# Score banks released one at a time, whole-row exponentials, and other queues for the router's stores

## Chip, cores and metric

One core of one Trainium2 chip runs the whole program. The metric is the time of one execution in device microseconds (us). The kernel before took 4668.68 us, the median of 3 runs (4661.94 to 4672.85).

## What is computed

A transformer block with latent attention, dilated attention and a 16-expert feed-forward, followed by two layers that hold three attentions each; width 1024, 1024 tokens, in later layers 256 context tokens more. All in float32. What the change touches is softmax attention and the router:

```python
s = einsum('bqhd,bkhd->bhqk', q, k) * scale        # scores of 128 queries against 1024 or 1280 keys
p = softmax(s, axis=-1)
o = einsum('bhqk,bkhd->bqhd', p, v)
...
h2 = rms_norm(x, g_ffn) * (1.0 + sc_m) + sh_m      # the router's features, gathered later by the experts
aff = softmax(einsum('bsd,de->bse', h2, w_router) + b_router)
gate, idx = top_k(swapaxes(aff, 1, 2), cap)        # each of 16 experts chooses 128 tokens
x = x + gt_m * expert_choice_ffn(h2, ...)
```

## The kernel before

The program is a row of stages; each is a block with its own instruction list per engine, and a barrier stands between two blocks.

**stage_attention** (from L891) is called five ways. Its names in the trace are `am` (latent attention, 1024 keys), `ad` (dilated attention, 1024 keys, with a bias), `aa` (difference maps, 1280 keys), `ab` (grouped queries, 1280 keys) and `ac` (neighbourhood, `apart=True`, up to 384 near keys and 256 context keys, with a bias). `aa`, `ab` and `ac` run once in each of the two layers. A step `h` is one head and one tile of 128 queries. Its scores lie in the PSUM buffer `ps[h % SB]` of `banks` banks of 512 columns. With 1024 keys `banks` is 2, `SB` (buffers) is 3 and `LAG` is 2; with 1280 keys `banks` is 3, `SB` is 2 and `LAG` is 1. Steps with all 1024 or 1280 keys number 64 in `am`, 64 in `ad`, 128 in `aa` and 96 in `ab` (both layers together); in the first of the two layers `aa` and `ab` also have short steps, for the context queries, with 256 keys.

What one step does, engine by engine. PE: `scores(h)` (L1052), then `transposes(h - LAG)` (L1062), which turns the probabilities 128 columns at a time back into the same PSUM buffer, then in every second step `turned` (L1087, one transpose), then half of `values` (L1078). DVE: in every second step the part that ends a pair of heads (L1127 to L1136: add the two partial denominators, reciprocal, two multiplications), then the row maximum of step h (L1146; in `ad` the bias and the maximum in one, L2226), then its share of copying the turned probabilities of step h - LAG from PSUM to `pT` (L1117). ACT: in every second step a copy of `po` to `oT` (L1161), then its share of the copy to `pT` (L1167), then two exponentials of step h, one for each of the two `spans` (L1178), each with a read of the accumulated denominator.

The spans are (0, 512) and (512, width). ACT copies `by_act`: the columns up to `(banks - 1) * 512`, so 512 of 1024 and 1024 of 1280, and in `ad` all 1024. DVE copies the rest, `by_dve`: 512 in `am`, 256 in `aa` and `ab`, none in `ad`. `scores(h)` overwrites the buffer of step h - SB, so it waits ahead of its first matmul for both copies of that step, `eva` (ACT) and `evd` (DVE), at L1047 and L1048. DVE credits `evd` after its copy, and in program order that copy stands behind the maximum of the step after next (`am`, `ad`) or the next (`aa`, `ab`). `transposes` waits for the first exponential (`ex0`, L1058) and ahead of column 512 for the second (`ex`, L1061); `tr0` tells ACT that its columns are turned, `tr` tells DVE.

**stage_router** (from L1339) goes over 8 tiles of 128 tokens. SP loads 8 weight chunks of 2 MB into 3 buffers (L1379) for a product with the conditioning that shares the stage (`mod_product`, L253). DVE makes the features `h2[:, t % 2]` of a tile (L1419, L1422), PE turns them (L1452), ACT copies them (L1397), PE forms the logits (L1462), ACT and DVE the softmax. The features of tile t reuse the buffer of tile t - 2, so DVE first waits for that tile's store (L1418). Both stores go out from POOL's queue, in this order for each tile: the store of `h2` to `h2_d` (L1475; `h_d` in the trace), a wait until it has landed (L1476), the store of the same tile of `x_sb` to `x_d` (L1477). The latter turns tokens into grid order: a tile is 2 grid rows of 64 tokens, and the transfer is [2 rows][64 tokens][1024], with tokens 64 KB apart in `x_d`. Nothing in the stage reads `x_d`; the block ends when all has landed (L1479). The stage after it, `stage_choose`, picks tokens on DVE.

## Time and profile before

| | |
|---|---|
| median of 3 runs | 4668.68 us |
| the profiled execution | 4670.11 us, of which the span is 4668.2 us |
| PE busy | 3658.2 us (78%) |
| DVE busy | 2452.2 us (53%) |
| ACT busy | 2213.7 us (47%) |
| POOL busy | 921.1 us (20%) |
| mean granted TensorE clock | 0.898 of full |
| `am`, `ad` | 492 to 765 us, 785 to 1035 us |
| router stage | 1141 to 1297 us |
| `aa`, `ab`, first of the two layers | 2475 to 2800, 2800 to 3050 us |
| `aa`, `ab`, last layer | 3890 to 4122, 4122 to 4342 us |

The profile shows the chip's own record of one execution. A busy share is an average over stages with different limits, so each stage is read alone: in the timeline of a few steps one looks for the work before which an engine sat idle, and for what released it (in brackets at a row's end). PE is TensorE's matmuls, PEld its weight loads, DVE VectorE, ACT ScalarE, POOL GpSimd; "ACTq L1182" as a releaser means ACT's queue at that line. The clock is 1.00 at TensorE's upper level, 2.4 GHz, and 0.50 at its lower, 1.2 GHz.

### The profile page before, as it was taken

The page shows a single profiled execution, that of the slowest core. Times are in us where ns is not written, and L with a number is a line of the kernel's source. Part 1 is how long each engine was busy: PE and PEld are TensorE (multiplying, and loading weights), DVE is VectorE, ACT ScalarE, POOL GpSimd, SP SyncE. Part 2 cuts the span into 40 slices and gives each one's busy share as a digit, 9 for nine tenths or more (in the row PEclk, how much of TensorE's full clock was granted, in tenths as well). Part 3 has the DMA queues.
Part 4 walks back from the last instruction along what each step waited for, and adds up shares of the span by engine and source line. Part 5 has one row for each costly group of instructions (what it writes and reads, how often), then busy time and mean ns, then how long its engine had stood idle before and what let it go on. Part 6 is the DMA issues. An engine that isn't in the chain of part 4 may idle for free. (4 is left out here: it accounts for less than half of the span.)

```text
span 4668.2 us, 70984 instructions
## 1 busy us (share of the span) xinstructions
PE 3658.2 (78%) x24823; PEld 2986.7 (64%) x24823; DVE 2452.2 (53%) x4546; ACT 2213.7 (47%) x3912; POOL 921.1 (20%) x748
## 2 busy tenths in 40 slices
PE   3987786888339999769996868865979968869558
PEld 3974565667327888558874657643768856658446
DVE  2114454443268878557544545555558745546455
ACT  2216454761017777542225656645442217657452
POOL 0214000000005656315550000000025540000002
PEclk7998898998669999879998989987989989989889
DMA  7237413412469999633323314061233332232433
GB/s 253 78 113 223 111 38 81 109 34 91 154 250 359 398 394 397 233 124 108 104 75 72 104 41 109 20 146 59 72 128 108 108 97 52 82 80 61 97 102 91
DMA packets 332951, 625.03 MB, mean 134 GB/s; under 512 B 122148, under 2 KB 178372, under 8 KB 331556
## 3 DMA queue, kind: packets, MB, share of 16 engines
q1 hardware_dynamic: 291360, 506.26, 34.2%
q0 software_dynamic: 39776, 108.71, 7.6%
q8 instruction: 209, 3.42, 0.3%
q10 hardware_dynamic: 1444, 5.30, 0.3%
q14 instruction: 162, 1.33, 0.1%
HBM read 486.20 MB, written 133.97 MB: 133 GB/s over the span
## 5 line engine op out<-in xcount | busy, mean ns | idle before, releaser
L1941 PE MATMUL pr_ps<-pr_wH,hT_part 128*128 128x512 f32 (+1 forms) x1120 | 428.6, 383 | 0.0
L1693 ACT ACTIVATE ex_high<-ex_ring 128x2048 fp32r<-128x2048 f32 x192 | 368.7, 1920 | 96.7 <-PE ex_pg L1669 41.2
L1739 DVE TENSOR_TENSOR ex_ring_part<-ex_ring,ex_high 128x2048 fp32r<-128x2048 f32 x144 | 372.9, 2589 | 51.4 <-ACTq L1694 39.6
L1941 PE MATMUL pr_ps<-pr_wH,x_sb_part 128*128 128x512 f32 x896 | 359.2, 401 | 20.9 <-DVEq L2017 20.9
L1941 PE MATMUL pr_ps<-pr_ws_part,x_sb_part 128*128 128x512 f32 x896 | 352.9, 394 | 0.0
L1146 DVE TENSOR_REDUCE aa_nm<-aa_ps 128x1 f32<-128x1280 f32 (+1 forms) x144 | 197.7, 1373 | 228.3 <-PE aa_ps L1052 227.6
L1634 POOL TENSOR_TENSOR ex_ring_part<-ex_ring,ex_high 128x2048 fp32r<-128x2048 f32 x48 | 239.5, 4989 | 217.2 <-ACTq L1694 217.2
L1062 PE MATMUL aa_ps<-ident,aa_prob 128*128 128x128 f32 x1312 | 208.6, 293 | 60.3 <-ACTq L1182 59.1
L1178 ACT ACTIVATE aa_prob<-aa_ps,aa_nm 128x512 f32<-128x512 f32 (+2 forms) x272 | 210.9, 775 | 87.6 <-DVEq L1147 45.4
L1146 DVE TENSOR_REDUCE ab_nm<-ab_ps 128x1 f32<-128x1280 f32 (+1 forms) x108 | 148.3, 1373 | 194.4 <-PE ab_ps L1052 193.9
L1941 PEld LDWEIGHTS pr_ps<-pr_wH,hT_part 128*128 128x128 f32 x1120 | 211.3, 189 | 44.6
L1262 PE MATMUL o_ps<-o_wH,o_yT 128*128 128x512 f32 x832 | 230.7, 395 | 0.0
L1062 PEld LDWEIGHTS aa_ps<-ident,aa_prob 128*128 128x128 f32 x1312 | 148.9, 147 | 112.7 <-ACTq L1182 106.1
L1941 PEld LDWEIGHTS pr_ps<-pr_wH,x_sb_part 128*128 128x128 f32 x896 | 169.4, 189 | 57.1 <-DVEq L2012 21.8
L1178 ACT ACTIVATE ab_prob<-ab_ps,ab_nm 128x512 f32<-128x512 f32 (+1 forms) x204 | 158.4, 776 | 95.7 <-DVEq L1147 69.9
L1941 PEld LDWEIGHTS pr_ps<-pr_ws_part,x_sb_part 128*128 128x128 f32 x896 | 169.5, 189 | 34.1
L1052 PE MATMUL ac_ps<-ac_kT,ac_qT 128*128 128x384 f32 (+1 forms) x204 | 75.0, 372 | 146.6 <-DVEq L1118 84.2
L1052 PE MATMUL aa_ps<-aa_kT,aa_qT 128*128 128x512 f32 (+1 forms) x400 | 121.8, 413 | 82.7 <-DMA aa_v<-proj 64.3
L1167 ACT ACTIVATE aa_pT<-aa_ps 128x1024 f32<-128x1024 f32 (+1 forms) x144 | 137.1, 952 | 83.0 <-PE aa_ps L1062 82.4
L1078 PE MATMUL aa_po<-aa_pT,aa_v 128*64 128x128 f32 x2624 | 176.4, 280 | 0.0
L1262 PEld LDWEIGHTS o_ps<-o_wH,o_yT 128*128 128x128 f32 x832 | 156.0, 190 | 31.4
L1178 ACT ACTIVATE ac_prob<-ac_ps,ac_nm 128x384 f32<-128x384 f32 (+1 forms) x204 | 104.3, 511 | 145.7 <-DVEq L1147 135.3
(358 smaller groups left out, 9001.6 us busy)
## 6 DMA issues: line engine op xcount, KB each, us to landing
ex_ring<-in_w_gate SPq DMA_DIRECT2D x64, 1024.0 KB, 10.2
ex_ring<-in_w_up SPq DMA_DIRECT2D x64, 1024.0 KB, 8.7
ex_ring<-in_w_down SPq DMA_DIRECT2D x64, 1024.0 KB, 8.4
z_d<-pr_zT POOLq DMA_DIRECT2D x120, 256.0 KB, 3.1
pr_ws<-in_w_in SPq DMA_DIRECT2D x14, 2048.0 KB, 9.1
mod_w<-in_w_ada SPq DMA_DIRECT2D x10, 2048.0 KB, 13.2
rt_mw<-in_w_ada SPq DMA_DIRECT2D x8, 2048.0 KB, 13.4
proj<-pr_raw POOLq DMA_DIRECT2D x54, 256.0 KB, 2.3
```

The costliest lines, as they stand in the source:

```text
L1052: mm = tensor.matmul(ps[h % SB][:, at:at + m], q.bitcast(F32R), kk.bitcast(F32R), start=i == 0, stop=i == len(ab) - 1)
L1062: mm = tensor.transpose(ps[h % SB][:, c:c + P], prob[:, h % SB, c:c + P], ident[:, :])
L1078: mm = tensor.matmul(po[j * dv:(j + 1) * dv, 0:P], v[:, p % 2, key, j * dv:(j + 1) * dv], pT[:, m % 2, j, at:at + P], start=c == 0, stop=c ...
L1146: vector.tensor_reduce(most, ps[h % SB][:, 0:count[t]], AX.X, ALU.max, negate=True)
L1167: scalar.activation(pT[:, g // 2 % 2, j, cols], ps[g % SB][:, cols], ACT.Copy)
L1178: scalar.activation(prob[:, h % SB, c0:c1], ps[h % SB][:, c0:c1], ACT.Exp, bias=nm[:, h % SB:h % SB + 1], scale=-1.0 if add_bias is not No ...
L1262: mm = tensor.matmul(ps[:, t % 2, cols], yT[:, t % 2, part, c, :].bitcast(F32R), w[:, c, cols].bitcast(F32R), start=c == 0 and i == 0, sto ...
L1634: pool.tensor_tensor(w_part[:, c % SL].bitcast(F32R), w_sb[:, c % SL], wH[:, c % HL], ALU.subtract)\
L1693: scalar.activation(wH[:, c % HL].bitcast(F32R), w_sb[:, c % SL], ACT.Copy)
L1739: vector.tensor_tensor(w_part[:, c % SL].bitcast(F32R), w_sb[:, c % SL], wH[:, c % HL], ALU.subtract)
L1941: mm = tensor.matmul(ps[:, g % 4, c0:c1], x.bitcast(F32R), w[:, i % WS, kk, c0:c1].bitcast(F32R), start=kk == 0 and m == 0, stop=kk == KC ...
```

## The change

Five edits to attention and two to the router.

1. The wait for `evd` moves from ahead of all of `scores(h)` to ahead of its columns from 512 on, where ACT's share is exactly columns 0 to 512 (`am`, `aa`, `ab`). Elsewhere (`ad`, `ac`, short steps) it stays ahead of the first matmul and is repeated ahead of each piece.
2. `by_act` with 1280 keys shrinks from 1024 columns to 512; DVE's share grows from 256 to 768.
3. New spans for the exponentials, `rises`: with 3 buffers (`am`, `ad`) one exponential of 1024; with 1280 keys one of 1024 and one of 256, in place of 512 and 768. `ac` keeps its two.
4. `transposes` waits for `ex` where the second rise starts: at column 1024 with 1280 keys, and not at all in `am` and `ad`.
5. The addition of two denominators (L1127) is dropped where there is one rise.
6. The router's `h2` stores go out from ACT's queue, after the copy of the turned features, with a semaphore for each of the two buffers.
7. The stores to `x_d` stay on POOL's queue, but are issued at once after `gd` (L1413), without a wait between them, 16 of one grid row each: [64 tokens][1024], 256 KB.

```diff
--- before.py
+++ after.py
@@ -931,10 +931,14 @@
         SB = 6 // banks
         LAG = SB - 1
 
+
+        rises = [s if apart or len(s) == 1 else [(0, s[-1][1])] if SB == 3 else
+                 [(0, (banks - 1) * 512), ((banks - 1) * 512, s[-1][1])] for s in spans]
+
         def by_act(t):
             if len(spans[t]) == 1 or (add_bias is not None and not apart):
                 return (0, spans[t][-1][1])
-            return spans[t][0] if apart else (0, (banks - 1) * 512)
+            return spans[t][0] if apart else (0, 512)
 
         def by_dve(t):
             c0, c1 = by_act(t)[1], spans[t][-1][1]
@@ -1043,10 +1047,12 @@
                         p, t, j = steps[h]
                         if t == 0 and j == 0:
                             pe.wait_ge(ld[p % 2], turn(it, p) * 16 * (n_loads + 2))
+
                         if h >= SB:
                             pe.wait_ge(eva, it * n + (h - LAG))
-                            pe.wait_ge(evd, it * n + (h - LAG))
                         for at, key, m in pieces(t):
+                            if h >= SB and (at == 512 or by_act(t) != (0, 512)):
+                                pe.wait_ge(evd, it * n + (h - LAG))
                             ab = passes(p % 2, j, t * P, key, m)
                             for i, (q, kk) in enumerate(ab):
                                 mm = tensor.matmul(ps[h % SB][:, at:at + m], q.bitcast(F32R), kk.bitcast(F32R),
@@ -1057,7 +1063,7 @@
                         t = steps[h][1]
                         pe.wait_ge(ex0, it * n + (h + 1))
                         for c, _ in chunks(t):
-                            if len(spans[t]) == 2 and c == spans[t][1][0]:
+                            if len(rises[t]) == 2 and c == rises[t][1][0]:
                                 pe.wait_ge(ex, it * n + (h + 1))
                             mm = tensor.transpose(ps[h % SB][:, c:c + P], prob[:, h % SB, c:c + P], ident[:, :])
                             if c + P == by_act(t)[1]:
@@ -1123,7 +1129,7 @@
                         if g % 2 and g >= 5:
                             m = (g - 5) // 2
                             p, t, _ = steps[2 * m]
-                            if len(spans[t]) == 2:
+                            if len(rises[t]) == 2:
                                 vector.tensor_tensor(den[:, m % RING, 0, :], den[:, m % RING, 0, :], den[:, m % RING, 1, :], ALU.add)
                                 dve.drain()
                             vector.reciprocal(rd[:, :], den[:, m % RING, 0, :])
@@ -1173,8 +1179,8 @@
                             if m >= RING:
                                 act.wait_ge(od, it * M + (m - RING + 1))
                             for x in range(2):
-                                if x < len(spans[t]):
-                                    c0, c1 = spans[t][x]
+                                if x < len(rises[t]):
+                                    c0, c1 = rises[t][x]
                                     scalar.activation(prob[:, h % SB, c0:c1], ps[h % SB][:, c0:c1], ACT.Exp,
                                                       bias=nm[:, h % SB:h % SB + 1],
                                                       scale=-1.0 if add_bias is not None else 1.0,
@@ -1341,8 +1347,9 @@
 
         n = "rt"
         ld, var, root, gd, kept = (sem(f"{n}_{s}") for s in ("ld", "var", "root", "gd", "kept"))
-        h_full, t_full, hT_full, lg, soft, ex, at_full, at_out, st, soft_out = (
-            sem(f"{n}_{s}") for s in ("h", "t", "hT", "lg", "max", "ex", "aT", "aTo", "st", "so"))
+        h_full, t_full, hT_full, lg, soft, ex, at_full, at_out, soft_out = (
+            sem(f"{n}_{s}") for s in ("h", "t", "hT", "lg", "max", "ex", "aT", "aTo", "so"))
+        st = [sem(f"{n}_st{j}") for j in range(2)]
 
         chunks = MOD_ROUTER
         NM = len(chunks)
@@ -1396,11 +1403,14 @@
                         act.wait_ge(lg, t)
                     scalar.activation(hT[:, :, :], tp[:, :, :], ACT.Copy)
                     act.drain().then_inc(hT_full, 1)
+                    act.dma_start(h2_d[t * P:(t + 1) * P, :], h2[:, t % 2, :]).then_inc(st[t % 2], 16)
                     act.wait_ge(soft, t + 1)
                     if t:
                         act.wait_ge(at_full, t)
                     scalar.activation(aff[:, :], lgt[:, :], ACT.Exp, bias=nm[:, 0:1], accum_out=den[:, 0:1])
                     act.drain().then_inc(ex, 1)
+                for j in range(2):
+                    act.wait_ge(st[j], 16 * (ST // 2))
 
             @block.vector
             def _(dve):
@@ -1415,7 +1425,7 @@
                 def features(t):
                     b = t % 2
                     if t >= 2:
-                        dve.wait_ge(st, 16 * (t - 1))
+                        dve.wait_ge(st[t % 2], 16 * (t // 2))
                     vector.scalar_tensor_tensor(h2[:, b, :], x_sb[:, t * D:(t + 1) * D], r[:, t:t + 1], gb[:, :],
                                                 ALU.mult, ALU.mult)
                     dve.drain()
@@ -1470,13 +1480,11 @@
             @block.gpsimd
             def _(pool):
                 pool.wait_ge(gd, 1)
-                for t in range(ST):
-                    pool.wait_ge(h_full, t + 1)
-                    pool.dma_start(h2_d[t * P:(t + 1) * P, :], h2[:, t % 2, :]).then_inc(st, 16)
-                    pool.wait_ge(st, 16 * (t + 1))
-                    pool.dma_start(x_d.rearrange("(c r) d -> r c d", r=ROWS)[t * P // GRID:(t + 1) * P // GRID],
-                                   x_sb[:, t * D:(t + 1) * D]).then_inc(kept, 16)
-                pool.wait_ge(kept, 16 * ST)
+                for r in range(ROWS):
+                    t, half = r // (P // GRID), r % (P // GRID)
+                    pool.dma_start(x_d.rearrange("(c r) d -> r c d", r=ROWS)[r],
+                                   x_sb[half * GRID:(half + 1) * GRID, t * D:(t + 1) * D]).then_inc(kept, 16)
+                pool.wait_ge(kept, 16 * ROWS)
 
     EX_RING = 11
```

## Rows read from the trace of the kernel before

**Rows 1.** Stretches: us, busy time by engine, granted clock, DMA share, GB/s

```profile
1141.00:1297.00 156.00, 56.11 (x712) 49.43 (x712) 33.69 (x72) 14.49 (x29) 11.02 (x16) 0.62 0.51 173
1271.00:1290.00 19.00, 0.00 (x0) 0.00 (x0) 0.00 (x0) 0.00 (x0) 0.82 (x1) 0.50 0.13 40
2500.00:2625.00 125.00, 107.09 (x1032) 80.93 (x1030) 69.99 (x136) 89.91 (x181) 0.97 (x1) 1.00 0.15 33
```

**Rows 2.** Router timeline: start us, us, engine, line, operation, [idle before <-releaser]

```profile
1163.37 3.09 PE L253 MATMUL rt_mp<-rt_mw,mod_c 128*32 128x128 f32 x64
...
1171.71 3.64 PE L253 MATMUL rt_mp<-rt_mw,mod_c 128*32 128x128 f32 x64
...
1184.67 0.56 POOL L1475 DMA_DIRECT2D h_d<-rt_h  x1
...
1201.10 1.28 DVE L1419 SCALAR_TENSOR_TENSOR rt_h<-x_sb,rt_r,rt_g 128x1024 f32<-128x1024 f32 x1 [9.52 <-DMA h_d<-rt_h]
```

**Rows 3.** Router timeline, its end

```profile
1260.71 1.95 PE L253 MATMUL rt_mp<-rt_mw,mod_c 128*32 128x128 f32 x64
...
1282.27 0.82 POOL L1477 DMA_DIRECT2D x_d<-x_sb  x1 [13.76 <-DMA h_d<-rt_h]
...
1297.77 0.39 SPq L1524 DMA_DIRECT2D ch_mw<-in_w_ada  x1
```

**Rows 4.** DMA issues of the page, POOL's queue: count, KB each, us to landing

```profile
proj<-pr_raw POOLq DMA_DIRECT2D x54, 256.0 KB, 2.3
```

**Rows 5.** Waits in am: for whom, us in total, times, longest

```profile
PE am_ps L1052 <- DVEq L1118: 18.6, 56, 1.4
```

**Rows 6.** Timeline of am, one round of the loop that sets its pace

```profile
605.81 1.63 PE L1052 MATMUL am_ps<-am_kT,am_qT 96*128 96x512 f32 x6 [0.34 <-DVEq L1118]
...
607.48 1.23 DVE L1146 TENSOR_REDUCE am_nm<-am_ps 128x1 f32<-128x1024 f32 x1 [1.84 <-PE am_ps L1052]
...
608.82 0.69 DVE L1117 COPY am_pT<-am_ps 128x512 f32<-128x512 f32 x1
...
609.68 1.63 PE L1052 MATMUL am_ps<-am_kT,am_qT 96*128 96x512 f32 x6 [0.24 <-DVEq L1118]
```

**Rows 7.** Instructions by tile: duration ns min/median/max, first and last start, forms

```profile
L1178 ACT ACTIVATION_READ_ACCUMULATOR am_prob<-am_ps,am_nm x128: 190/193/195, 497.6 to 749.8; 128x1 f32 x128
...
L1178 ACT ACTIVATE aa_prob<-aa_ps,aa_nm x272: 473/690/902, 2482.5 to 4111.0; 128x512 f32<-128x512 f32 x128, 128x256 f32<-128x256 f32 x8
```

**Rows 8.** Timeline of ad, two steps

```profile
852.99 0.19 PEld L1052 LDWEIGHTS ad_ps<-ad_kT,ad_qT 128*128 128x128 f32 x1 [0.35 <-ACTq L1168]
...
855.40 1.02 ACT L1167 ACTIVATE ad_pT<-ad_ps 128x1024 f32<-128x1024 f32 x1
...
856.66 0.19 PEld L1052 LDWEIGHTS ad_ps<-ad_kT,ad_qT 128*128 128x128 f32 x1 [0.17 <-ACTq L1168]
...
858.76 1.02 ACT L1167 ACTIVATE ad_pT<-ad_ps 128x1024 f32<-128x1024 f32 x1 [0.46 <-PE ad_ps L1062]
```

**Rows 9.** Timeline of aa, two steps

```profile
2600.93 0.85 PE L1052 MATMUL aa_ps<-aa_kT,aa_qT 128*128 128x512 f32 x3
...
2603.68 0.42 DVE L1117 COPY aa_pT<-aa_ps 128x256 f32<-128x256 f32 x1 [0.37 <-PE aa_ps L1062]
...
2605.82 1.49 DVE L1146 TENSOR_REDUCE aa_nm<-aa_ps 128x1 f32<-128x1280 f32 x1 [0.55 <-PE aa_ps L1052]
...
2606.65 0.87 PE L1062 MATMUL aa_ps<-ident,aa_prob 128*128 128x128 f32 x6 [0.43 <-ACTq L1182]
...
2607.34 1.02 ACT L1167 ACTIVATE aa_pT<-aa_ps 128x1024 f32<-128x1024 f32 x1 [0.77 <-PE aa_ps L1062]
...
2608.70 0.86 PE L1052 MATMUL aa_ps<-aa_kT,aa_qT 128*128 128x512 f32 x3
```

**Rows 10.** Timeline of ab: the first matmul of scores, two steps apart

```profile
2901.30 0.50 PE L1052 MATMUL ab_ps<-ab_kT,ab_qT 128*128 128x512 f32 x1
...
2908.94 0.50 PE L1052 MATMUL ab_ps<-ab_kT,ab_qT 128*128 128x512 f32 x1
```

## Prediction

> **What bounds the kernel now.** I read the stretches first, because the change touches stages with different limits, and then in each stage a timeline of two or three steps, looking for the idle time ahead of an engine's work and its releaser.
>
> The router stage takes 156 us, PE is busy for 56 of them, the DMA engines for half, at a clock of 0.62 [rows 1]. It is a chain of stores. POOL issues the store of one tile's features at 1184.67, and DVE starts the features of the next tile but one at 1201.10, after 9.52 us of idleness that ended when that store landed [rows 2]: one tile in 16 to 18 us. Why is a store of 512 KB so slow? At 1282.27 the last store to `x_d` goes out, into an empty machine, and the next stage starts at 1297.77 [rows 3]; from 1271 to 1290 the DMA share is 0.13 at 40 GB/s [rows 1]. That is 2 engines of 16. So the `x_d` store of a tile, shaped [2][64][1024], is cut in two and takes some 14 us whatever else goes on, and the feature store of the next tile stands behind it in POOL's queue.
>
> In `am` one loop closes: scores 1.63, 0.04 to the maximum, 1.23, 0.11, the copy 0.69, 0.17, scores again, 3.87 us in all [rows 6]. PE idles for the end of that copy 56 times, 18.6 us in total [rows 5]. In `ad` ACT and PE pass the step to each other: ACT's copy takes 1.02 and scores start 0.08 to 0.24 after it, at 856.66; the next copy starts 2.10 later [rows 8]. The other step, from 852.99 to 856.66, is 3.67 long because its copy starts only 2.41 after the scores, ACT being busy with exponentials and `oT`. In `aa` two steps take 7.77 us, 3.885 each [rows 9]. ACT goes round: exponentials of 512 and 768, wait 0.77 for the turned columns, copy 1024. PE waits 0.43 for the second exponential in each step. DVE has room. In `ab` two steps take 7.64 us, 3.82 each, and scores start with no idle time ahead of them [rows 10]: scores have two passes there, and PE is the bound.
>
> **The change, part by part.**
>
> Router, edits 6 and 7. Three chains remain. First the tiles themselves. Where no store held them back, product 0 to product 1 took 8.34 us (1163.37 to 1171.71) [rows 2]: DVE's two feature operations, PE's transposes, the product, and DVE's row sum, all at a low clock. The product took 3.09 and 3.64 there but 1.95 at the end, once PE had been busy for a while [rows 2, 3]. I take 8.0 us. Six such rounds and a shorter one of 5 (it makes no features: 8.0 less two operations like the 1.28 of [rows 2] and their gaps) put product 7 at 1163.4 + 48 + 5 = 1216.4. Before it stood at 1260.7 [rows 3]. From there to the end of the block I allow 6 us for the last row sum, four small stores and the barrier: 1222. Second the `x_d` stores. A 256 KB store on POOL's queue lands in 2.3 us in another stage [rows 4], so 16 of them are tens of microseconds of one sixteenth-spread queue, beside 6 MB of weights; they are over by about 1180. Third the `h2` stores. Each goes out about a copy of 1024 columns after its transposes (1.02 in `ad` [rows 8]), and its buffer is wanted 13 us after them (features t + 2), so it has over 11 us; nothing is ahead of it on ACT's queue, and what is behind it is the softmax's exponential, for which ACT now idles anyway. An issue costs 0.56 on POOL [rows 2]; the trace has none of this size on ACT, so 0 to 0.8 us each, on no path. The one thing that could hurt is the flood at the start: 4 MB of stores on top of 6 MB of weights. I allow 2 us. The block then ends at 1224 in place of 1297.8: **74 us less**, 62 to 84 by tile rounds of 9.0 or 6.5 us and 0 to 4 us for the flood.
>
> The Trainium skill, "DMA: Bandwidth & Descriptors", section on why a DMA increments its semaphore by 16, says that the number of DMA engines is the largest up to 16 that divides the slowest dimension of both sides: 2 before, 16 after. The share of 0.13 [rows 1] agrees for the old shape; no row has the new one. The same page, "Issuing engines are not separate DMA queues", speaks against edit 6: moving a store to another issuer saves issue time only. By that rule alone edit 6 would give nothing; the rows show the time lost in the order within POOL's queue and its narrow neighbour, which edits 6 and 7 both end.
>
> `am`, edits 1, 3, 5. The first half of scores no longer waits for DVE, so PE's 18.6 us go [rows 5]. What is late next is PE. DVE's loop now holds half the scores: 0.82 + 0.04 + 1.23 + 0.11 + 0.69 + 0.17 = 3.06, under PE's own 3.87 less some 0.3, 3.55. One exponential of 1024 delays the first transposes of a step, but they come two steps later. It shortens ACT, which isn't late. **18 us**, 8 to 20.
>
> `ad`, edits 3, 5. The waits stay. Exponentials of 256, 512 and 768 take 473, 690 and 902 ns [rows 7], 0.212 us for each 256 columns, so 1024 take 1.115. Two of 512 and two reads of the accumulator (0.193) become one and one: 1.38 + 0.39 - 1.115 - 0.19 = 0.46 us less on ACT per step. In the long step ACT's copy then starts when the columns are turned, 2.10 after the scores as in the other step, and scores follow at 3.2 to 3.3 in place of 3.67 [rows 8]. In the short step ACT waits 0.46 for PE already, and nothing is won. 0.39 us in each of 32 pairs: **12 us**, 0 to 14.
>
> `aa`, edits 1 to 4. Four durations are new. Copies on DVE: 256 columns take 0.42 [rows 9], 512 take 0.69 [rows 6], so 768 take 0.96. ACT's copy falls from 1.02 to about 0.6. The exponentials keep their sum (512 + 768 = 1024 + 256), and the last one no longer stands between PE and most of its transposes: those of eight chunks need only the first. So PE's 0.43 and ACT's 0.77 [rows 9] both shrink, and ACT leaves the path. DVE comes onto it. Even step: the 768 columns of scores that wait, 0.57 (0.85 for 1280 [rows 9] less 0.28 for the first 512, an estimate by columns), 0.04, maximum 1.49, 0.11, copy 0.96, 0.17, together 3.34. Odd step: DVE does the pair's end between copy and maximum. It takes 1.17 now (from 2604.10, the copy's end, to 2605.27, where the 0.55 of idleness begin [rows 9]); 1.49 + 0.11 + 0.96 + 1.17 + 0.1 = 3.83. The pair is 7.17, 3.585 a step. PE needs 7.77 - 0.86 = 6.91 and stays under that. 0.30 us in 128 steps: **38 us**; the two ends are PE's own bound, 0.43 each and 55 us, and 17 us if the early first bank brought nothing (rivals).
>
> `ab`, the same edits. PE has little idle time to give, a tenth of a microsecond in some steps at the `ex` wait by my estimate. DVE's loop: the waiting part of scores is 768 columns twice, as much as the half of `am`'s, 0.82; with the 2.77 of everything behind it 3.59 in the even step, 3.83 in the odd one, 3.71 together, below 3.82 but by 0.11 only. **3 us**, from a loss of 10 to a gain of 8. `ac` gets one satisfied wait more per step, ahead of a matmul queued behind a running one: 0, up to a loss of 3.
>
> Sum against the profiled execution: 74 + 18 + 12 + 38 + 3 = 145; 4670.1 - 145 = **4525 us**. That execution was 1.4 us above the median shown, so the same number stands for the median.
>
> **Rivals.**
>
> A, DVE takes the bound in `aa` and `ab` entirely. If starting the first bank early brings nothing (the matmuls of a step are held together by something else), the loop has all the scores again: `aa` 0.85 + 2.77 = 3.62 and 3.83, mean 3.73, so 20 us are won instead of 38; `ab`, five sixths of `am`'s scores, 1.36 + 2.77 = 4.13, a loss of 0.31 in 96 steps, 30 us. Time 4525 + 18 + 33 = 4576. For it: DVE's margin in `ab` is 0.11 us. Against it: nothing in the program ties the banks together.
>
> B, the `x_d` stores don't spread. If a store of one grid row uses two engines again, 16 of them in one queue still need 8 times 14 = 112 us from ten microseconds before product 0 on, and the block ends at 1266: 32 us won in place of 74, 4567 us. This is the case in which edit 7 doesn't do what it says. Against it: the store of [rows 4] with many outer rows lands in 2.3 us.
>
> C, more than forecast: PE runs at the upper level in the router (rounds of 6.5 us, 9 us more) and is the bound in `aa` (17 more): 4499.
>
> D, slower than before. The clock: it stands at 1.00 in `aa` with PE busy 107 of 125 us, and at 0.62 in the router with 56 of 156 [rows 1]. If PE, now waiting in the middle of scores on top of ahead of transposes, were granted 0.50 in attention, a step of 3.8 us with some 3.4 of PE work would take about 7, 3.2 more. It decides from 45 such steps of 352 on (145 / 3.2). Against it: PE's waits get shorter in total, not longer.
>
> **How the numbers follow.** Forecast 0.74, A 0.09, B 0.07, C 0.09, D 0.01. Own ranges: the terms' ends added as independent errors give about 25 us to each side of 4525. The range takes in B and A: 4492 to 4582. About 0.2% (9 us) is what a measurement of this kernel can tell from no change. Every case but D is far beyond that: faster 0.98, same 0.01, slower 0.01.
>
> **What would show it.** In the router: eight rounds of 7 to 9 us, no DVE wait for `h_d`, a block of some 83 us, and `x_d` stores landing within 30 us of the first issue. In `am`: no wait for L1118 left, steps of 3.55 to 3.6. In `ad`: both steps 3.2 to 3.3. In `aa`: steps of 3.34 and 3.83, DVE's copy 0.96, and a PE wait for DVE's copy in the middle of scores. In `ab`: 3.8 as before. The prediction is wrong if the router's gain is under 60 us, or if `ab` becomes slower than 3.9 a step.

## The result, and the profile after

The changed kernel takes 4503.37 us, the median of 4 runs (4501.89 to 4505.05), beside 4666.97 us for the kernel before on the same chip; the ratio is 0.9649, with a 95% interval of 0.9632 to 0.9666. The forecast was 4525 us, its range 4492 to 4582. The profiled execution took 4502.05 us, 168.1 less than the one shown of before, where the sum of the prediction said 145. Of all executions below one ran in a slower state of the chip (`split_same_reg`, 4923.15 us at a granted clock of 0.749); no figure includes it.

Busy times on the page of the changed kernel (engine, us, share of the span, instructions):

```profile
span 4499.9 us, 70349 instructions
PE 3621.7 (80%) x24823; PEld 2979.1 (66%) x24823; DVE 2568.7 (57%) x4482; ACT 2074.7 (46%) x3656; POOL 922.5 (20%) x748
```

ACT gives 139 us of work away, DVE takes 117 more. PE's share hardly moves; what goes is idle time. Where it goes is read stage by stage. For an attention stage the figure is the time from the start of its first row maximum to that of its last (in `ac` of the first layer, to the last with near keys). For the router it is the time from the issue of the block's first load to the issue of the next block's first load of large weights. Digits 0 and 1 are the first and the last layer. The figures are taken from the profiled executions, one of each kernel; a gain is worked out before rounding.

| stage | before | after | gain | forecast |
|---|---|---|---|---|
| `am` | 251.3 | 231.9 | 19.4 | 18 |
| `ad` | 227.3 | 212.0 | 15.3 | 12 |
| router | 156.2 | 81.9 | 74.2 | 74 |
| `aa` 0 + 1 | 548.0 | 509.9 | 38.2 | 38 |
| `ab` 0 + 1 | 386.9 | 376.4 | 10.5 | 3 |
| `ac` 0 + 1 | 303.5 | 299.6 | 3.9 | 0 |
| all the rest | 2795.0 | 2788.2 | 6.8 | 0 |

**Router.** Stretches of the block in the changed kernel; the columns are those of [rows 1], the last two the DMA share and GB/s:

```profile
1115.00:1125.00 10.00, 6.07 (x28) 5.70 (x29) 5.36 (x6) 2.32 (x3) 8.48 (x16) 0.50 1.05 390
1125.00:1135.00 10.00, 8.55 (x160) 7.48 (x159) 4.13 (x10) 2.84 (x6) 0.00 (x0) 0.88 1.03 413
...
1155.00:1165.00 10.00, 8.49 (x122) 7.50 (x114) 5.49 (x11) 1.43 (x3) 0.00 (x0) 0.83 1.05 395
1165.00:1183.00 18.00, 14.62 (x243) 12.75 (x243) 7.59 (x21) 3.25 (x8) 0.00 (x0) 0.81 0.59 228
```

Against 0.51 of [rows 1] the DMA share is 1.03 to 1.05 for fifty microseconds. The tail at a share of 0.13 is gone. The products of its timeline on PE:

```profile
1126.18 2.54 PE L253 MATMUL rt_mp<-rt_mw,mod_c 128*32 128x128 f32 x64
...
1133.09 1.96 PE L253 MATMUL rt_mp<-rt_mw,mod_c 128*32 128x128 f32 x64
...
1143.86 3.64 PE L253 MATMUL rt_mp<-rt_mw,mod_c 128*32 128x128 f32 x64 [3.51 <-DMA rt_mw<-in_w_ada]
...
1180.27 1.96 PE L253 MATMUL rt_mp<-rt_mw,mod_c 128*32 128x128 f32 x64
```

Eight products, 54.1 us from the first to the last start. DVE waits for no `h_d` any more; PE waits once, for weights. The `x_d` stores, from the view of the DMA issues in that stretch:

```profile
L1485 POOL DMA_DIRECT2D x_d<-x_sb x16: 532/539/578, 1115.2 to 1123.2; - x16
...
DMA to landing us min/median/max: 6.6/11.4/18.5
```

**`am`.** Two steps of the timeline (start, duration, engine, line, what waited for what); compare [rows 6]:

```profile
640.68 1.23 DVE L1152 TENSOR_REDUCE am_nm<-am_ps 128x1 f32<-128x1024 f32 x1 [0.55 <-PE am_ps L1058]
...
642.02 0.69 DVE L1123 COPY am_pT<-am_ps 128x512 f32<-128x512 f32 x1
...
642.47 1.66 PE L1058 MATMUL am_ps<-am_kT,am_qT 96*128 96x512 f32 x6
...
644.16 1.23 DVE L1152 TENSOR_REDUCE am_nm<-am_ps 128x1 f32<-128x1024 f32 x1 [1.45 <-PE am_ps L1058]
...
647.76 1.23 DVE L1152 TENSOR_REDUCE am_nm<-am_ps 128x1 f32<-128x1024 f32 x1 [0.52 <-PE am_ps L1058]
```

Scores at 642.47 start while DVE's copy, 642.02 to 642.71, still runs. The maxima are 3.48 and 3.60 apart, in place of 3.87. The wait for DVE's copy (L1118 in [rows 5], L1124 now) has no row left among PE's waits in the stage.

**`ad`.** Maxima at 860.67 and 863.92, 3.25 apart. Over the stage they are 3.20 and 3.29 apart in turn, in place of 3.67 and 3.21 around [rows 8]:

```profile
860.67 1.23 DVE L2234 CUSTOM_DVE_ANT_0 ad_ps<-ad_ps,logc 128x1024 f32<-128x1024 f32 x1 [1.93 <-PE ad_ps L1058]
...
861.39 1.02 ACT L1173 ACTIVATE ad_pT<-ad_ps 128x1024 f32<-128x1024 f32 x1 [0.20 <-PE ad_ps L1068]
...
862.54 0.50 PE L1058 MATMUL ad_ps<-ad_kT,ad_qT 128*128 128x512 f32 x1
...
863.92 1.23 DVE L2234 CUSTOM_DVE_ANT_0 ad_ps<-ad_ps,logc 128x1024 f32<-128x1024 f32 x1 [0.95 <-PE ad_ps L1058]
```

ACT's copy now waits 0.20 for the turned columns: here ACT has stopped being late.

**`aa`, last layer.** DVE's timeline over a pair, and PE's row of the second part of scores:

```profile
3811.86 0.61 PE L1058 MATMUL aa_ps<-aa_kT,aa_qT 128*128 128x512 f32 x2 [0.54 <-DVEq L1124]
...
3812.51 1.49 DVE L1152 TENSOR_REDUCE aa_nm<-aa_ps 128x1 f32<-128x1280 f32 x1 [0.73 <-PE aa_ps L1058]
...
3814.12 0.96 DVE L1123 COPY aa_pT<-aa_ps 128x768 f32<-128x768 f32 x1
...
3815.20 0.16 DVE L1133 TENSOR_TENSOR aa_den<-aa_den 128x2 f32<-128x2 f32 x1
...
3815.76 0.48 DVE L1142 TENSOR_SCALAR aa_o<-aa_pf,aa_rd 128x64 f32<-128x64 f32 x2 [0.16 <-issue]
...
3816.43 1.49 DVE L1152 TENSOR_REDUCE aa_nm<-aa_ps 128x1 f32<-128x1280 f32 x1 [0.19 <-issue]
...
3819.74 1.49 DVE L1152 TENSOR_REDUCE aa_nm<-aa_ps 128x1 f32<-128x1280 f32 x1 [0.74 <-PE aa_ps L1058]
```

The two steps are 3.92 and 3.31. The maximum at 3816.43 waits for nothing but DVE itself, because the end of the pair stands ahead of it: DVE has come onto the path, as forecast. PE now waits 0.54 in the middle of scores, for DVE's copy (L1124).

**`ab`.** DVE's maxima (2759.89, 2763.55, 2767.39) are 3.66 and 3.84 apart, over the whole stage 3.70 and 3.80; before 3.70 and 3.93.

### The profile page after: what moved, and what is told of

Its sections match the earlier page's. It is cut to its first block and busy times, and to the rows that moved or that the text cites. A ratio compares the mean times of both kernels' runs of the same rounds, so it can differ in the third digit from the quotient of the medians.

```text
span 4499.9 us, 70349 instructions
## 1 busy us (share of the span) xinstructions
PE 3621.7 (80%) x24823; PEld 2979.1 (66%) x24823; DVE 2568.7 (57%) x4482; ACT 2074.7 (46%) x3656; POOL 922.5 (20%) x748
## 5 line engine op out<-in xcount | busy, mean ns | idle before, releaser
L1184 ACT ACTIVATE aa_prob<-aa_ps,aa_nm 128x256 f32<-128x256 f32 (+1 forms) x272 | 211.1, 776 | 137.8 <-DVEq L1153 120.5
L1058 PE MATMUL aa_ps<-aa_kT,aa_qT 128*128 128x512 f32 (+1 forms) x400 | 144.6, 439 | 111.5 <-DMA aa_v<-proj 63.8
L1184 ACT ACTIVATE ab_prob<-ab_ps,ab_nm 128x1024 f32<-128x1024 f32 (+1 forms) x204 | 158.4, 776 | 129.3 <-DVEq L1153 117.4
L1949 PEld LDWEIGHTS pr_ps<-pr_wH,x_sb_part 128*128 128x128 f32 x896 | 169.5, 189 | 56.2 <-DVEq L2020 20.8
L1068 PE MATMUL aa_ps<-ident,aa_prob 128*128 128x128 f32 x1312 | 174.9, 281 | 10.9 <-ACTq L1188 10.9
L1058 PEld LDWEIGHTS aa_ps<-aa_kT,aa_qT 128*128 128x128 f32 x400 | 69.4, 199 | 167.3 <-DMA aa_v<-proj 64.6
L1268 PEld LDWEIGHTS o_ps<-o_wH,o_yT 128*128 128x128 f32 x832 | 156.2, 190 | 31.5
L1084 PE MATMUL aa_po<-aa_pT,aa_v 128*64 128x128 f32 x2624 | 175.1, 279 | 0.0
L1058 PE MATMUL ab_ps<-ab_kT,ab_qT 128*128 128x512 f32 (+1 forms) x300 | 121.0, 403 | 64.2 <-DMA ab_v<-proj 58.5
```

The costliest lines, as they stand in the source:

```text
L1058: mm = tensor.matmul(ps[h % SB][:, at:at + m], q.bitcast(F32R), kk.bitcast(F32R), start=i == 0, stop=i == len(ab) - 1)
L1068: mm = tensor.transpose(ps[h % SB][:, c:c + P], prob[:, h % SB, c:c + P], ident[:, :])
L1084: mm = tensor.matmul(po[j * dv:(j + 1) * dv, 0:P], v[:, p % 2, key, j * dv:(j + 1) * dv], pT[:, m % 2, j, at:at + P], start=c == 0, stop=c ...
L1184: scalar.activation(prob[:, h % SB, c0:c1], ps[h % SB][:, c0:c1], ACT.Exp, bias=nm[:, h % SB:h % SB + 1], scale=-1.0 if add_bias is not No ...
L1268: mm = tensor.matmul(ps[:, t % 2, cols], yT[:, t % 2, part, c, :].bitcast(F32R), w[:, c, cols].bitcast(F32R), start=c == 0 and i == 0, sto ...
L1949: mm = tensor.matmul(ps[:, g % 4, c0:c1], x.bitcast(F32R), w[:, i % WS, kk, c0:c1].bitcast(F32R), start=kk == 0 and m == 0, stop=kk == KC ...
```

## The experiments

In all of them a stage's figure is taken as in the table above. Kernels with one execution each are read stage by stage, because totals of one kernel differ between executions: those of the kernel before went from 4660.0 to 4674.3 us in one set of 11. The time at which `am` begins alone lies between 493 and 501 us.

### wait_ahead: edit 1 undone

```diff
-                            if h >= SB and (at == 512 or by_act(t) != (0, 512)):
+                            if h >= SB and (at == 0 or by_act(t) != (0, 512)):
                                 pe.wait_ge(evd, it * n + (h - LAG))
```

> The changed kernel with edit 1 undone: the wait for VectorE's copy stands ahead of all scores again, everything else as changed. My theory (the loop scores, maximum, copy, scores closes on VectorE, and the early first bank is what takes half or a third of the scores out of it): am back to 3.87 us a step, 19 us longer in all; aa's short round 3.31 grows to 3.6 and its long one stays at 3.9, so 0.15 a step and about 19 us; ab 4.1 in both steps, 0.35 a step and about 34 us; 4502 + 72 = 4574 us. The rival (the gain in aa and ab came from the narrower copy on ScalarE and the later second exponential, and where the wait stands decides nothing): am 19 us longer, aa and ab unchanged, 4521 us.

Measured: 4596.29 us. `am` 251.4, all of its gain gone; `aa` 283.6 and 251.9; `ab` 219.7 and 197.2, slower than before by 11.5 and 18.5. One step of `ab`:

```profile
2820.89 1.49 DVE L1152 TENSOR_REDUCE ab_nm<-ab_ps 128x1 f32<-128x1280 f32 x1 [1.60 <-PE ab_ps L1058]
...
2822.50 0.96 DVE L1123 COPY ab_pT<-ab_ps 128x768 f32<-128x768 f32 x1
...
2823.63 0.47 PE L1058 MATMUL ab_ps<-ab_kT,ab_qT 128*128 128x512 f32 x1 [0.33 <-DVEq L1124]
...
2825.06 1.49 DVE L1152 TENSOR_REDUCE ab_nm<-ab_ps 128x1 f32<-128x1280 f32 x1 [0.52 <-PE ab_ps L1058]
```

The whole of a loop can be read off: maximum, copy, then all of scores, 1.39, and the next maximum, 4.17 us. In `aa` the steps are 3.60 and 3.91. So the larger share for DVE (edit 2) needs the freed bank: without edit 1 the others bring 12.5 us in `aa` and lose 30.0 in `ab`. Rival A had priced this case at a gain of 20 and a loss of 30; its mechanism is right, and edit 1 is what prevents it. The total came out 22 us above the 4574 expected. Beside the changed kernel `aa` lost 25.6 where 19 were expected, `ab` 40.5 where 34 were, and `ad`, which this run leaves as it is, was 4.1 longer; the rest lies at the beginning and in the router.

### two_rows: edit 7 half undone

```diff
-                for r in range(ROWS):
...
-                                   x_sb[half * GRID:(half + 1) * GRID, t * D:(t + 1) * D]).then_inc(kept, 16)
+                for t in range(ST):
+                    pool.dma_start(x_d.rearrange("(c r) d -> r c d", r=ROWS)[t * P // GRID:(t + 1) * P // GRID],
+                                   x_sb[:, t * D:(t + 1) * D]).then_inc(kept, 16)
```

> The changed kernel with the old shape of the x_d stores: 8 stores of [2 rows][64 tokens][1024], still issued at once and without waits, features still from ScalarE's queue. Theory of the prediction (each such store uses 2 DMA engines, one after another in one queue, 14 us each): the router's block ends 112 us after the first issue in place of 70, at 45 us longer, 4546 us. Rival (each store takes another pair of engines, so eight of them run side by side and 14 to 20 us see them all landed; then the waits between the stores were the cost, and the new shape is worth nothing here): block unchanged at 82 us, 4502 us. The Trainium skill, DMA: Bandwidth & Descriptors, section on why a DMA increments its semaphore by 16, states for POOL's queue a round-robin cursor over the engines; that is the rival.

Measured: 4514.85 us, router block 94.4, so 12.5 more than after and far below what my theory said. The landing of the eight stores, from the view of their issues:

```profile
DMA to landing us min/median/max: 14.9/35.4/57.8
```

Three stretches of the block, in the columns as above:

```profile
1115.00:1125.00 10.00, 4.88 (x22) 4.51 (x22) 6.10 (x5) 2.31 (x2) 6.31 (x8) 0.50 1.07 372
...
1145.00:1155.00 10.00, 7.18 (x81) 6.46 (x81) 0.57 (x2) 0.00 (x0) 0.00 (x0) 0.50 1.02 318
1155.00:1165.00 10.00, 2.83 (x25) 2.37 (x29) 3.25 (x6) 1.42 (x3) 0.00 (x0) 0.50 0.98 262
```

DVE's timeline, the features of tile 4 (counted from 0), which wait for the store of tile 2:

```profile
1155.21 1.28 DVE L1429 SCALAR_TENSOR_TENSOR rt_h<-x_sb,rt_r,rt_g 128x1024 f32<-128x1024 f32 x1 [5.44 <-DMA h_d<-rt_h]
```

Eight stores of the old shape would need 8 times 14 = 112 us if they ran in turn; the last landed within 58 us of its issue, so they ran side by side. The DMA engines are as busy as with the new shape (a share of 0.98 to 1.11), but move 262 to 372 GB/s while the stores are under way, where the new shape has 390 to 413. PE waits for weights twice, 2.47 and 4.29 us. The Trainium skill, "DMA: Bandwidth & Descriptors", section on why a DMA increments its semaphore by 16, says that a store of POOL's queue that uses fewer than 16 of the DMA engines takes consecutive ones from a cursor that moves on. The trace agrees in that all of them are busy here; rival B had been priced without this sentence. With no waits between the stores, and `h2` on ACT's queue, the old shape costs 12.5 us. That doesn't tell what the waits would cost with the new shape, since no run has the two together. In the kernel before, the `h2` stores of the router, from the view of their issues, landed in

```profile
DMA to landing us min/median/max: 7.4/15.2/19.7
```

The 7.4 is the first, the only one with no `x_d` store ahead of it on its queue; the seven behind one took 13.9 to 19.7. So each wait was long because a store of the old shape stood in front. An estimate: with the waits kept and the new shape, that 7.4 and two issues of 0.54 make rounds of some 8.5 us, so the shape alone might have brought most of the gain as well.

### h2_on_pool: edit 6 undone in its queue alone

```diff
-                    act.dma_start(h2_d[t * P:(t + 1) * P, :], h2[:, t % 2, :]).then_inc(st[t % 2], 16)
...
+                for t in range(ST):
+                    pool.wait_ge(h_full, t + 1)
+                    pool.dma_start(h2_d[t * P:(t + 1) * P, :], h2[:, t % 2, :]).then_inc(st[t % 2], 16)
```

> Edit 6 undone in part: the h2 stores go back to POOL's queue, behind all 16 x_d stores and without the wait after each; the x_d stores and the two semaphores stay as in after. Theory (what counted was the wait that stood between the stores and the narrow neighbour; the issuing queue itself counts for nothing while the DMA engines are full with weights anyway): DVE's features wait a little for h_d, but product 2 waits for its weights in any case; the block keeps its 82 us to within 5, total 4502 to 4509. Rival (ACT's queue is needed, because stores behind 4 MB on one queue land late): the first h2 store lands only behind the last x_d store, 30 us or more after its issue, features 2 start some 15 to 20 us late and the block is 95 to 100 us, total 4515 to 4522.

Measured: 4510.05 us, router block 88.7. The first lines are the features of tile 2 and then PE's row behind them:

```profile
1141.25 1.28 DVE L1426 SCALAR_TENSOR_TENSOR rt_h<-x_sb,rt_r,rt_g 128x1024 f32<-128x1024 f32 x1 [10.46 <-DMA h_d<-rt_h]
...
1143.92 1.97 PE L1459 MATMUL rt_tp<-ident,rt_h 128*128 128x128 f32 x8 [12.00 <-DVEq L1430]
```

Between the two expectations: the store of tile 0, behind 4 MB on its queue, keeps DVE waiting 10.46 us once. The block is only 6.8 longer than in the changed kernel, since PE has no wait for weights left in it. DVE waits for no other store. ACT's queue is worth 6 to 7 us here, for one store.

### router_only: edits 6 and 7 alone

```diff
+                            pe.wait_ge(evd, it * n + (h - LAG))
                         for at, key, m in pieces(t):
-                            if h >= SB and (at == 512 or by_act(t) != (0, 512)):
-                                pe.wait_ge(evd, it * n + (h - LAG))
...
-                            if len(rises[t]) == 2 and c == rises[t][1][0]:
+                            if len(spans[t]) == 2 and c == spans[t][1][0]:
```

> The kernel before with edits 6 and 7 alone. Theory (the parts add up, for a barrier stands between the stages): router block 82 us instead of 156, every attention stage as before; total 4670 - 74 = 4596. Rival (attention is disturbed or helped by how the router ends, so the sum is not the sum of its parts): total off 4596 by over 9 us.

Measured: 4596.77 us, router block 82.3, `am` 252.1, `ad` 227.9, `aa` 290.1 and 257.0, `ab` 208.5 and 178.9. Each stage of attention is within 1.7 us of before. The parts add up, as expected.

### spans_again: edits 3, 4 and 5 undone

```diff
-        rises = [s if apart or len(s) == 1 else [(0, s[-1][1])] if SB == 3 else
-                 [(0, (banks - 1) * 512), ((banks - 1) * 512, s[-1][1])] for s in spans]
+        rises = spans
```

> The changed kernel with edit 3 undone in full: exponentials of 512 and the rest everywhere, the wait for the second of them at column 512, the denominators added everywhere. Theory: am unchanged, because its transposes come two steps later; ad loses its 15 us again; aa and ab unchanged within 3 us, because the columns are turned 0.7 us before VectorE's copy wants them, so a TensorE stall of 0.4 in the middle of the transposes costs nothing while VectorE is the bound in aa; ab up to 5 us longer. 4502 + 15 + 3 = 4520 us. Rival (TensorE is within 0.1 us of the bound in aa's short round, so the stall comes back in each of them, 0.4 us in 64): 26 us more in aa, 4545 us.

Measured: 4524.1 us. `ad` is 222.5, 10.4 longer. `am` (232.9), `ab` (200.6 and 175.4) and `aa` (269.0 and 237.5) don't notice. The exponentials pay where ACT is the bound, in `ad`, and nowhere else. Of the other 12 us in the total 7.3 are the beginning: `am` starts that much later, in a stretch that the edit doesn't touch.

### old_shares: edit 2 undone

```diff
-            return spans[t][0] if apart else (0, 512)
+            return spans[t][0] if apart else (0, (banks - 1) * 512)
...
-                            if h >= SB and (at == 512 or by_act(t) != (0, 512)):
+                            if h >= SB and (at == (banks - 1) * 512 or apart or by_act(t) != (0, (banks - 1) * 512)):
```

> Edit 2 undone alone: with 1280 keys ACT copies 1024 columns again and DVE 256, and scores wait for DVE's copy only ahead of column 1024; the exponentials of 1024 and 256 stay. Theory (ACT's loop of exponentials and a copy of 1.02 us becomes the bound of aa, about 3.8 a step instead of 3.31/3.91): aa loses some 10 us in each layer, ab is bound by PE and keeps its 3.75, total about 4522. Rival (ACT isn't on the path, the whole gain of aa came from the freed banks and the exponentials' order): aa stays within 3 us of after in each layer, total 4498 to 4506.

Measured: 4527.57 us. `aa` 280.1 and 247.1, together 17.3 more than after; `ab` 203.9 and 175.1. A step of `aa` in the last layer:

```profile
3813.09 1.02 ACT L1173 ACTIVATE aa_pT<-aa_ps 128x1024 f32<-128x1024 f32 x1
...
3814.34 1.11 ACT L1184 ACTIVATE aa_prob<-aa_ps,aa_nm 128x1024 f32<-128x1024 f32 x1 [0.22 <-issue]
...
3815.62 1.31 PE L1068 MATMUL aa_ps<-ident,aa_prob 128*128 128x128 f32 x10 [0.20 <-ACTq L1188]
```

Steps of 3.52 and 3.85: the exponential waits for ACT's own copy, the transposes for the exponential. Without edit 2 ACT is the bound, as expected. So `aa` gains 20.8 us without edit 2 and 12.5 without edit 1, in place of 38.2: the two edits need each other.

### split_end and split_same_reg: what holds `aa` now

If DVE's odd step is long because it holds the whole end of a pair (1.17 us), half of that end belongs in the even step:

```diff
-                    for h in range(n + 4 + LAG):
+                    for h in range(n + 5 + LAG):
...
                             dve.drain()
+                        if g % 2 == 0 and g >= 6:
+                            m = (g - 6) // 2
+                            p, t, _ = steps[2 * m]
```

> A new version: VectorE's end of a pair is split over two steps, the addition and the reciprocal in one, the two multiplications in the next. Theory (in aa the step that holds the 1.17 us of a pair's end is bound by VectorE, 3.91, while in the other VectorE idles 0.74 us waiting for scores): both steps of aa become 3.3 to 3.4, 0.6 us less a pair, 50 full pairs and more, about 33 us; am, ad and ab, which TensorE or ScalarE bound, stay within 3 us; 4502 - 33 = 4469 us. Rival (TensorE's own work in aa is 3.5 us a step, as the prediction had it, 6.91 a pair): 3.46 a step, 0.15 us, 20 us in all, 4482 us.

Measured: 4479.65 us, `aa` 262.8 and 230.7 (16.4 less than after), `ac` 150.7 and 138.5 (10.4 less). Steps of `aa` in the last layer:

```profile
3801.65 0.16 DVE L1133 TENSOR_TENSOR aa_den<-aa_den 128x2 f32<-128x2 f32 x1
...
3802.27 1.49 DVE L1155 TENSOR_REDUCE aa_nm<-aa_ps 128x1 f32<-128x1280 f32 x1 [0.21 <-PE aa_ps L1058]
...
3805.03 0.47 DVE L1145 TENSOR_SCALAR aa_o<-aa_pf,aa_rd 128x64 f32<-128x64 f32 x2 [0.19 <-issue]
...
3805.69 1.49 DVE L1155 TENSOR_REDUCE aa_nm<-aa_ps 128x1 f32<-128x1280 f32 x1 [0.19 <-PE aa_ps L1058]
```

Both halves fit into gaps in which DVE waited for scores anyway, and the steps are 3.30 and 3.43. This shows that DVE's order, not its busy time, set `aa`'s 3.91. The pair is 6.73, below the rival's 6.91, so PE's own work was less than the prediction had it. The amount was missed: 33 us were expected in `aa`. Half came, in part because three of its four regions began slowly in this execution (below); and `ac`'s 10.4 stood in neither forecast.

In the first layer the same steps are longer by 0.07 (3.37 and 3.50), as they are in the changed kernel (3.38 and 3.99 against 3.31 and 3.91). DVE's timeline of the changed kernel, the copy in the first layer and in the last:

```profile
2481.51 0.96 DVE L1123 COPY aa_pT<-aa_ps 128x768 f32<-128x768 f32 x1 [0.19 <-issue]
...
3814.12 0.96 DVE L1123 COPY aa_pT<-aa_ps 128x768 f32<-128x768 f32 x1
```

The copies are alike, but in the first layer DVE issues for 0.19 ahead of one that waits for nothing, where 0.12 lie between maximum and copy in the last. There the wait for the turned columns counts other steps than the other waits do (short steps don't count), so its value has to be computed in each step. `split_same_reg` lets every step count:

```diff
+                            elif not by_dve(t) and c == 0:
+                                mm.then_inc(tr, 1)
...
-                                dve.wait_ge(tr, it * parts_before(n) + parts_before(g + 1))
+                                dve.wait_ge(tr, it * n + (g + 1))
```

> split_end (the end of a pair of heads moved on DVE so that its two halves lie in different steps) and, besides, the semaphore of the turned columns counted in every step, so that DVE waits for tr against the same value as for its other waits and computes no second one in the layer whose streams have short steps. Theory (that computation of 0.07 us in each step of aa's first layer lies on DVE's loop): the steps of that layer go from 3.37 and 3.50 to 3.30 and 3.43, as in the last layer; 4.5 us less than split_end, about 4475. Rival (it is hidden, or the difference between the layers has another cause): 4479 as split_end, steps of aa's first layer unchanged.

Measured in 5 rounds: 4471.57 us, the median of five executions, ratio to before 0.9579 (0.9567 to 0.9592). The steps of the first layer are 3.31 and 3.43, as in the last: the cause is shown. The stages say less: `aa` 0 is 262.0 beside 262.8, because this execution began that stage with slower steps, and `aa` 1 is 223.9 beside 230.7 for the opposite reason (below).

### x_d_paced and paced_and_split: the flood

```diff
                     t, half = r // (P // GRID), r % (P // GRID)
+                    if half == 0:
+                        pool.wait_ge(h_full, t + 1)
                     pool.dma_start(x_d.rearrange("(c r) d -> r c d", r=ROWS)[r],
```

> The 16 x_d stores of after, two of them held back until the features of their tile are made, so that the 4 MB no longer go out at once on top of the weights. Theory (the flood costs only the wait of 3.51 us that PE has for its weights ahead of the third product, and the block is bound by the sum of its bytes behind that): the third product waits less than 1.5 us, but the weights of later products come later, and the block stays within 3 us of 82 (79 to 85), total about 4502. Rival 1 (the flood delays everything behind it): block 3 to 5 us shorter, about 4499. Rival 2 (the last x_d stores now land last of all, at the end of the block): block 85 or more, total 4505 or more.

Measured: 4504.01 us, router block 78.3; the products on PE's timeline:

```profile
1128.05 2.58 PE L253 MATMUL rt_mp<-rt_mw,mod_c 128*32 128x128 f32 x64
...
1142.20 3.64 PE L253 MATMUL rt_mp<-rt_mw,mod_c 128*32 128x128 f32 x64
...
1178.77 1.96 PE L253 MATMUL rt_mp<-rt_mw,mod_c 128*32 128x128 f32 x64
```

The wait for weights is gone, and my theory that the weights behind would come later instead has fallen: 50.7 us from first to last product, 7.25 a round. The first rival holds for the block, 3.7 us shorter: the bytes had fitted all along, and their order cost. The total doesn't show it (`aa` 1 was 2.9 longer in this execution). The same edit on top of `split_same_reg`:

> split_same_reg with the x_d stores held back to their tiles as in x_d_paced. Theory (the two gains lie in different blocks and add): router block 78 instead of 81.5, total 4473 - 3.6 = 4469.5. Rival (the 3.6 us of x_d_paced are the noise between executions, since that kernel's own total was no shorter than after's): router block 81 to 83, total 4473.

Measured in 5 rounds: 4470.63 us, ratio 0.9568 (0.9555 to 0.9581), router block 79.4. The totals' intervals overlap with those of `split_same_reg`, so they alone decide nothing. By blocks it holds, if narrowly: four executions with paced stores (the two runs below among them) took 78.3, 79.4, 80.8 and 80.6, seven with the same router but all stores at once 80.9 to 83.5, mean 82.4. That is 2.6 us by the means.

### warm_start and warm_until_loads: the clock at the start of a block

Unlike starts had shown up between executions of the same `aa` code: in the changed kernel the third and fourth full step of `aa` in the last layer took 3.31 and 3.30, in `x_d_paced`, with the same attention, 4.22 and 5.02. Scores of the third step on PE's timeline, `split_end` and then `split_same_reg`:

```profile
3703.78 1.01 PE L1058 MATMUL aa_ps<-aa_kT,aa_qT 128*128 128x512 f32 x2 [0.65 <-DVEq L1124]
```

```profile
3707.78 0.62 PE L1058 MATMUL aa_ps<-aa_kT,aa_qT 128*128 128x512 f32 x2 [0.65 <-DVEq L1126]
```

Both rows are the second part of the scores of the third step, 7.77 and 7.78 us after PE's first matmul of the block, which started at a clock of 0.50 in both. In one they take 1.01, in the other 0.62, the time at the upper level. The steps around them are 4.22 and 5.03 in one, 3.30 and 3.31 in the other. (Between these two the wait value differs, but `paced_and_split`, with the attention of the second, has 4.22 and 4.86.) Could PE be warmed up while it waits for its operands?

```diff
+                for _ in range(60):
+                    tensor.transpose(ps[0][:, 0:P], ident[:, :], ident[:, :])
```

> paced_and_split, and at the start of each of the 8 attention blocks PE turns the identity matrix 60 times into the first score buffer (14 us at 0.23 each at a clock of 0.50) while it waits for its first operands. The work is extra and its output is overwritten. Theory (the first scores of a block run at a clock of 0.50, and how soon the clock rises differs from run to run by 3 us or more a block): in all blocks the first scores take 0.25 a matmul in place of 0.4 to 0.5, the steps behind them 3.3 at once in place of 5.3 to 5.7, 4.2, 5.0; 3 to 5 us less a block, 24 to 40 in all, about 4440. Rival 1 (the clock falls again in the few us between the last of the 60 and the first scores, or the extra work delays them): no gain or a loss, 4465 to 4480. Rival 2 (the start of a block is held by loads of operands that land one after another, not by PE): first steps as long as before at a clock of 1.00, 4465 to 4470.

Measured in 5 rounds: 4471.77 us, ratio 0.9574 (0.9561 to 0.9588), no gain over `paced_and_split`. Stretches of the start of `aa` in the last layer, in the columns as above:

```profile
3679.00:3689.00 10.00, 9.61 (x60) 9.44 (x60) 0.00 (x0) 1.28 (x1) 0.00 (x0) 0.68 0.81 186
3689.00:3696.00 7.00, 0.05 (x1) 0.00 (x0) 0.00 (x0) 0.00 (x0) 0.00 (x0) 0.73 1.17 210
3696.00:3702.00 6.00, 3.89 (x13) 3.10 (x14) 2.98 (x2) 2.01 (x5) 0.00 (x0) 0.50 1.04 220
```

The clock rose in the turns (0.68 on average), and after 7.25 us of idleness the first scores ran at 0.50 again. So the turns were made to fill the wait, 108 in `aa`:

```diff
-                for _ in range(60):
+                for _ in range({"am": 140, "ad": 155, "aa": 108, "ab": 150, "ac": 165}[name[:2]]):
```

> warm_start with as many turns of the identity as fill the whole wait for the first operands at 0.141 us each: 140 in am, 155 in ad, 108 in aa, 150 in ab, 165 in ac, in place of 60. Theory (in warm_start the clock had risen and fell again in the 7 to 18 us of idleness that were left): the first scores of a block run at a clock of 1.00, six matmuls of aa's first two steps in 1.25 to 1.5 us instead of 2.50, and the steps behind them take 3.3 at once; 2 to 5 us less a block, 16 to 40 in all against paced_and_split, 4430 to 4455. Rival (something else makes the start slow, or what PE gains waits for DVE and ACT, or the turns outlast the loads): within 5 us of 4470.

Measured in 5 rounds: 4472.7 us, ratio 0.9569 (0.9553 to 0.9585). The rival holds: the total gains nothing. The loads landed later than I had reckoned, 3.3 to 6.4 us after the last turn, except in `am` (1.44). In `aa` of the last layer, with 4.50 us of idleness between them, scores began at the lower level:

```profile
3686.54 2.50 PE L1060 MATMUL aa_ps<-aa_kT,aa_qT 128*128 128x512 f32 x6 [4.50 <-DMA aa_v<-proj]
...
3694.32 1.01 PE L1060 MATMUL aa_ps<-aa_kT,aa_qT 128*128 128x512 f32 x2 [0.65 <-DVEq L1128]
```

In `ac` of the last layer, 3.25 us after the turns, they began at the upper one (a first matmul of 0.39, against 0.58 in `warm_start`), and the stage took 139.1 beside 138.1 without turns. `am` and `ad` (4.30 us after the turns) began at the upper level too, with a first matmul of 0.50 against 0.80, and took 233.2 and 213.7 beside 231.5 and 213.3: where a start was at full clock, the stage wasn't shorter. `aa` 0 was 5 to 6 us shorter in both kernels with turns (256.8 and 255.4, beside 261.9), though its scores began or fell back to the lower level there; whether the turns do this, these single traces don't tell. What a whole start at full clock would be worth to `aa` stays open: no run had one.

## Why the prediction was right

The forecast was 22 us too high; the time lies within the range. The terms left out or too small (`ab`, `ac`, the rest, `ad`) all err the same way. Point by point:

**Router, right in size and in its steps.** The block is 74.2 shorter, 74 was said. Last product to end: 5.6 us (1180.27 to 1185.82), 6 allowed. `x_d` stores: the last issue is at 1123.2 and the longest landing 18.5, so all had landed 27 us after the first issue; "within 30". First to last product: 54.1 for 53, or 55 with the 2 us for the flood. That the term fits to 0.2 us is luck, for it had two errors that cancel: a round without the flood takes 7.25 in place of 8.0, while the one wait for weights is 3.51 where I allowed 2; over the whole block the flood costs 2.6 by `x_d_paced`. The cause as given, a narrow store and behind it the next tile's, was right as a pair. What the runs split off is one-sided: with the waits gone the shape is worth 12 us (`two_rows` against the mean of 82.4) and ACT's queue 6. The other 55 or so belong to the waits and the shape together, and no run with the waits kept and the new shape divides them. Rival B was overpriced: it supposed turn-taking on two engines, and eight stores of that shape had all landed within 64 us of the first issue.

**`am`, right.** 19.4 for 18; steps of 3.48 and 3.60 for 3.55 to 3.6, and `wait_ahead` shows that edit 1 is the whole of it.

**`ad`, right.** 15.3 for 12; steps of 3.20 and 3.29 where both were to be 3.2 to 3.3. `spans_again` gives 10.4 of it back and has the old steps of 3.67. The other 4.8 lie at the beginnings of its two regions, outside the sum: with the old exponentials, too, the third and fourth step took 4.09 and 3.21 in place of 4.97 and 3.78, and the pause between the regions 16.5 in place of 18.3. The pause is scatter: in `x_d_paced`, with the same attention, it is 17.9. The steps may be too, for in `wait_ahead`, with the same `ad`, the second region had 5.06 and 4.04; whether another edit has a part in them, no run tells.

**`aa`, right, with a compensation.** The sum held to 0.2 us, which is luck again. Steps of 3.31 and 3.91 in the last layer for 3.34 and 3.83: the odd step was 0.08 too short in the sum, for the end of the pair and its gaps take 1.35 between copy (ends 3815.08) and maximum (3816.43), not 1.27. In the first layer each step takes 0.07 more, which nothing in the sum had. Against that stands what I had left out, the short steps of the context queries and their neighbours. Per layer the gain is 19.1 and 19.1. Two reasons given for `aa` don't hold. The prediction let the later second exponential shorten PE's and ACT's waits, but with the old exponentials `aa` takes 506.5 (`spans_again`), no more than with the new: edits 1 and 2 are the cause. And PE's need of 6.91 a pair was too high, since `split_end` has pairs of 6.73. The lower end of the term, 17, doesn't follow from rival A's own steps either, which give 20.

**`ab`, mis-sized.** 10.5 for 3. The bound stays with PE, and DVE's margin is thin (`wait_ahead`: 4.17). The 3.82 read from one pair [rows 10] was right as a mean, for the stage's steps alternate 3.70 and 3.93. What was too small is the gain in each: 0.03 a step was allowed, an estimate of PE's wait for the second exponential, and the long step went from 3.93 to 3.80, 0.065 a step. That is 6 us in 96 steps; the remaining 4 lie at the short steps and starts. Which edit shortens the long step stays open: it is 3.80 both in `spans_again` and in `old_shares`.

**`ac` and the rest, left out.** 3.9 and 6.8, neither in the sum. The time between the first and the last maximum of `ac` has no edit in it but a satisfied wait, and other executions gave `ac` 156.1 to 159.4 in the first layer with the changed kernel's `ac`, beside 156.7 here and 160.2 before, so some of the 3.9 is scatter. The 6.8 may be of the same kind: stretches that no edit touches, like the one ahead of `am`, which ended anywhere from 493 to 501 us.

**The rivals.** A did not occur, but its mechanism and its price for `ab` appear once edit 1 is taken away (4.17 a step for 4.13, 30.0 us for 30). B did not. C said 4499 for another reason: rounds of 6.5 us and PE as the bound of `aa`. The time is near its own, yet neither of its two conditions held; rounds were 7.25, and `aa` stayed with DVE. D did not: the clock's mean rose from 0.898 to 0.905.

## What to carry to other kernels

A wait ahead of a step's first matmul that only its second PSUM bank needs closes a loop through the slowest reader; placed ahead of that bank it took 64 steps from 3.87 to 3.54 us, and it made a larger share for that reader affordable, which alone would have lost 30 us in `ab`. Where slow stores are strung together by waits, look at both: here the shape cost 12 us once the waits were gone, and together with them and the shared queue 74. A run with the waits alone is what this case lacks. And where an engine bounds a loop by the order of its work, count gaps, not busy time: moving half of the end of a pair into the other step was worth 27 us in `aa` and `ac` with the same work.

## What the hardware showed that I had not expected

- Eight stores of the two-engine shape, issued at once on POOL's queue, moved 262 to 372 GB/s together with the weights; a lone one had left the machine at 40 [rows 1].
- When all waits of DVE go by the same count, a step is 0.07 us shorter than when one of them goes by a count of its own, which has to be computed (3.38 to 3.31).
- The same attention code at the same place is at the upper clock 8 us after PE's first matmul in one execution and not in another, and a region of `aa` then differs by about 3 us. After 4.50 us of idleness `aa` began at the lower level again; after 3.25 us `ac` and after 4.30 us `ad` began at the upper one, and `ad` fell back after four matmuls (0.39, then 0.58 and 0.63).
